# Mixture-of-experts stage of a two-block network: a split scatter, and another order of work where one expert ends and the next begins

## The reference, cut to what matters

```python
def _moe(x, w_router, w1, w3, w2):              # x: 256 x 1024
    logits = xt @ w_router                      # 8 experts, top 2 of each token
    gates = softmax(top_v)
    # for each expert: its tokens, in order
    h = silu(xg @ w1[e]) * (xg @ w3[e])         # 1024 -> 3584
    y[tokens] += (h @ w2[e]) * gate             # 3584 -> 1024
```

## Time and profile before

| what | value |
|---|---|
| median of 3 runs | 2785.34 us (2784.81 to 2785.59) |
| the profiled execution's own time | 2790.09 us |
| its span, first to last instruction | 2787.9 us |
| PE busy | 2699.8 us (97%) |
| DVE busy | 2113.8 us (76%) |
| ACT busy | 1631.4 us (59%) |
| mean granted TensorE clock | 0.996 |

### The profile page before, as it was taken

One profiled execution on the slowest core, in us unless ns is written; L12 is line 12 of the kernel. 1 busy time (PEld: TensorE's weight loads), 2 busy tenths in 40 slices (PEclk: granted clock), 3 DMA queues, 4 the chain that ended last, 5 costly groups with the idle time before them and its releaser, 6 DMA issues.

```text
span 2787.9 us, 44756 instructions
## 1 busy us (share of the span) xinstructions
PE 2699.8 (97%) x19124; PEld 2300.6 (83%) x19124; DVE 2113.8 (76%) x2117; ACT 1631.4 (59%) x1639; POOL 144.9 (5%) x152
## 2 busy tenths in 40 slices
PE   8999999999999999999999999999889999998999
PEld 7977898897788787887878787878678988877997
DVE  6677655657788888898989898877666866866685
ACT  4555443455467677676767676746545654654563
POOL 1000000000000000000000000000420000051000
PEclk9999999999999999999999999999999999999999
DMA  6345454544479898988988999953114445312443
GB/s 220 136 155 182 178 185 168 180 151 157 144 266 349 343 346 342 349 343 328 357 333 340 341 355 348 361 198 123 67 59 173 183 175 179 122 63 85 168 181 106
DMA packets 90510, 616.16 MB, mean 221 GB/s; under 512 B 10704, under 2 KB 10960, under 8 KB 20656
## 3 DMA queue, kind: packets, MB, share of 16 engines
q1 hardware_dynamic: 85392, 598.61, 58.0%
q0 software_dynamic: 4896, 14.36, 2.2%
HBM read 611.88 MB, written 1.05 MB: 220 GB/s over the span
## 4 chain that ended last, share of the span: by engine, by line
PE 82%; DVE 11%; ACT 4%; issue 2%; DMA 0%; SPq 0%; DVEq 0%; ACTq 0%
PE ps L701 24%; PE ps L703 23%; PE ps L702 23%; DVE wlo L1741 3%; ACT whi L1323 1%; PE ps L1006 1%; PE ps L1037 1%; PE ps L1183 1%; PE ps L1027 1%; ACT s L1626 1%; PE ps L1162 1%; PE ps L1194 1%; DVE s L2110 0%; DVE cin L2447 0%; ACT Q L1706 0%
## 5 line engine op out<-in xcount | busy, mean ns | idle before, releaser
L1741 DVE TENSOR_TENSOR wlo<-raw,whi 128x2048 fp32r<-128x2048 f32 (+3 forms) x588 | 1305.7, 2226 | 413.8 <-ACT whi L1323 405.4
L1323 ACT ACTIVATE whi<-raw 128x2048 fp32r<-128x2048 f32 (+3 forms) x588 | 1092.6, 1860 | 401.0 <-PE ps L703 385.2
L701 PE MATMUL ps<-whi,xTh 128*128 128x512 f32 (+5 forms) x1464 | 573.0, 391 | 12.7 <-issue 5.1
L703 PE MATMUL ps<-whi,xTl 128*128 128x512 f32 (+5 forms) x1464 | 563.2, 385 | 0.0
L702 PE MATMUL ps<-wlo,xTh 128*128 128x512 f32 (+5 forms) x1464 | 563.1, 385 | 0.0
L701 PE MATMUL ps<-xTh,whi 128*128 128x256 f32 x1480 | 418.1, 282 | 0.0
L703 PE MATMUL ps<-xTh,wlo 128*128 128x256 f32 x1480 | 417.4, 282 | 0.0
L702 PE MATMUL ps<-xTl,whi 128*128 128x256 f32 x1480 | 417.3, 282 | 0.0
L701 PEld LDWEIGHTS ps<-whi,xTh 128*128 128x128 f32 x1464 | 278.0, 190 | 73.3 <-issue 11.2
L703 PEld LDWEIGHTS ps<-whi,xTl 128*128 128x128 f32 x1464 | 277.6, 190 | 57.8
L702 PEld LDWEIGHTS ps<-wlo,xTh 128*128 128x128 f32 x1464 | 278.2, 190 | 53.3
(11 more groups left out here) (561 smaller groups left out, 3477.7 us busy)
## 6 DMA issues: line engine op xcount, KB each, us to landing
raw<-in_units_dram SPq DMA_DIRECT2D x544, 1024.0 KB, 5.0
raw<-in_units_dram SPq DMA_DIRECT2D x18, 512.0 KB, 3.6
raw<-in_units_dram SPq DMA_DIRECT2D x6, 768.0 KB, 7.1
raw<-in_units_dram SPq DMA_DIRECT2D x8, 544.0 KB, 3.6
raw<-in_units_dram SPq DMA_DIRECT2D x6, 688.0 KB, 4.0
g<-in_b_gate_dram POOLq DMA_DIRECT2D x16, 256.0 KB, 8.4
raw<-in_units_dram SPq DMA_DIRECT2D x4, 576.0 KB, 4.5
mk<-in_c_dn_dram POOLq DMA_DIRECT2D x2, 576.0 KB, 9.7
```

The costliest lines, as they stand in the source:

```text
L701: self.e.matmul(out, ah, bh, start=start, stop=False)
L703: return self.e.matmul(out, al, bh, start=False, stop=stop)
L1323: self.e.activation(self.m.hi[u % NHL][:, 0:n], self.m.raw[u % NRAW][:, 0:n], ACT.Copy) \
L1741: self.e.tensor_tensor(self.m.lo[u % NHL][:, 0:n], self.m.raw[u % NRAW][:, 0:n], self.m.hi[u % NHL][:, 0:n].bitcast(F32), ALU.subtract) \
```

## The change

1. The scatter is split like the weight products. `sel` (0/1, exact) is turned instead of `selg`, into `selT` (two buffers, fp32r). The result of `e2` is written as a high part (ACT, `expert_high`) and a low part (DVE, `expert_low`) into the first 8 blocks of `hTe`, and a scatter is four fp32r matmuls of 512 columns. The gate is multiplied in by DVE, which does the addition to `y` as two `scalar_tensor_tensor` of 128x512. `select` makes one selection (two instructions) instead of two (four). For the first column block of `e2` the two parts are written in a new step, `rest`, after the second unit of the second block.
2. The gather of the next expert leaves its place ahead of `e2` and goes to the end of the expert, in halves of 16 matmuls (first four blocks of 128 rows, then the last four). The new order at the end of expert ex is: last unit, first half of the gather, scatter 0, opening of the next expert, scatter 1, second half of the gather, branch. The opening waits for the first half of the gather alone; the second unit waits for the rest. ACT copies both parts of the second half, DVE the low part of the first.
3. `turn` stands between the first and the second unit of an expert.
4. Splits: the second unit's split of the next expert (call the units b0, b1, b2 ...) is held back from the last `e2` unit to the opening, and that of b2 is moved ahead, to just before DVE's and ACT's part of scatter 1.
5. Counts: PE reads 3, 3 and 2 counts at three steps around the last router products; DVE reads its eight at the start of `route`.

```diff
+    def expert_sum(self, cb):
+        return [h[:, 4 * cb:4 * cb + 4, :].rearrange("p (t a) n -> p t (a n)", t=2) for h in self.hTe]
...
+            if step[0] == "u" and step[1][0] == "e2" and step[1][1] < 7 and step[1][2] == 1 and step[2] == 6:
+                hold = 1
+            elif step[0] == "open" and step[1]:
+                hold = 0
+            elif step[0] == "scatter" and step[2] == 1 and step[1] < 7:
+                hold = -1
+            elif step[0] == "begin":
+                hold = 0
+            self.end.append(len(self.units) + (step[0] == "soon") - late - hold - AHEAD * (step[0] == "embed"))
...
-            o += [("counts",)] + pr[2][1:2] + [("gather", 0)]
+            o += [("counts",)] + pr[2][1:2] + [("counted",)]
+            o += [("gather", 0, 0), ("open", 0), ("gather", 0, 4)]
...
-            o += [("begin", ex), ("turn", ex)]
+            o += [("begin", ex)]
...
+                o += e1 if cb else e1[0:1] + [("turn", ex)] + e1[1:2]
...
-            if ex < 7:
-                o += [("gather", ex + 1), ("across", ex, 6)]
-            n = 3 if ex == 7 else 7
-            if ex == 7:
-                o += e2[0][0:1] + [("across", 7, 6)]
-            o += e2[0][ex == 7:] + e2[1][0:n] + [("scatter", ex, 0)] + e2[1][n:] + [("scatter", ex, 1), ("finish", ex)]
+            o += e2[0][0:1] + [("across", ex, 6)] + e2[0][1:] + e2[1][0:2] + [("rest", ex, 0)] + e2[1][2:4]
+            if ex < 7:
+                o += e2[1][4:] + [("gather", ex + 1, 0), ("scatter", ex, 0), ("open", ex + 1), ("scatter", ex, 1)]
+                o += [("gather", ex + 1, 4)]
+            else:
+                o += [("scatter", ex, 0)] + e2[1][4:] + [("scatter", ex, 1)]
+            o += [("finish", ex)]
... (PE)
+    def counts(self, first, last):
+        if first == 0:
+            self.e.wait_ge(*self.at("cnt"))
+            self.count = []
+        for ex in range(first, last):
+            self.count.append(self.e.value_load(self.m.cnt[0:1, ex:ex + 1], min_val=0, max_val=256))
...
     def scatter(self, ex, cb):
-        ps = self.fill(("sc", ex, cb), ("y", ex, cb))
-        e.wait_ge(*self.at("selgT", ex))
+        ps, T = self.fill(("sc", ex, cb), ("y", ex, cb)), m.selT[ex % 2]
+        high, low = m.expert_sum(cb)
+        e.wait_ge(*self.at("selT", ex))
+        e.wait_ge(*self.at("hiT", "ev", "e2", ex, cb))
+        for q in range(2):
+            for s in range(self.tiles):
+                e.matmul(ps[:, q * 512:q * 512 + 512], T[:, s, q * 128:q * 128 + 128], high[:, s, :], start=(s == 0), stop=False)
         e.wait_ge(*self.at("ev", "e2", ex, cb))
         for q in range(2):
             for s in range(self.tiles):
-                ins = e.matmul(ps[:, q * 512:q * 512 + 512], m.selgT[:, s, q * 128:q * 128 + 128], m.hb[:, cb, s, :],
-                               start=(s == 0), stop=(s == self.tiles - 1))
+                ins = e.matmul(ps[:, q * 512:q * 512 + 512], T[:, s, q * 128:q * 128 + 128], low[:, s, :], start=False,
+                               stop=(s == self.tiles - 1))
... (ACT)
+            ex, d0 = a
+            for half in ((1, 0) if d0 else (0,)):
...
+    def expert_high(self, ex, cb):
+        g, n = ("e2", ex, cb), self.tiles
+        self.e.wait_ge(*self.at("full", *g))
+        self.e.activation(self.m.expert_sum(cb)[0][:, 0:n, :], bands(self.psum(*g))[:, 0:n, :], ACT.Copy) \
+            .then_inc(*self.up("a_moe", ("hiT", "ev") + g))
... (DVE)
+            ex, d0 = a
+            if d0 == 0:
+                key = ("xg", ex, 1, 0)
+                e.wait_ge(*self.at("full", *key))
+                e.tensor_copy(m.xT[1][:, 0:4, :], bands(self.psum(*key), 4)).then_inc(*self.up("d_moe", key))
...
-            e.tensor_tensor(yy, yy, bands(self.psum("sc", *a)), ALU.add).then_inc(*self.up("d_moe", ("y",) + a))
+            for t in range(2):
+                ins = e.scalar_tensor_tensor(yy[:, t, :], bands(self.psum("sc", *a))[:, t, :], m.gate[:, t, a[0]:a[0] + 1],
+                                             yy[:, t, :], ALU.mult, ALU.add)
+            ins.then_inc(*self.up("d_moe", ("y",) + a))
...
+    def expert_low(self, ex, cb):
+        g, n, (high, low) = ("e2", ex, cb), self.tiles, self.m.expert_sum(cb)
+        self.e.wait_ge(*self.at("hiT", "ev", *g))
+        self.e.tensor_tensor(low[:, 0:n, :], bands(self.psum(*g))[:, 0:n, :], high[:, 0:n, :].bitcast(F32), ALU.subtract) \
+            .then_inc(*self.up("d_moe", ("ev",) + g))
...
         for t in range(2):
-            e.tensor_scalar(m.selg[:, t, :], m.iota[:, :], m.pos[:, t, ex:ex + 1], m.gate[:, t, ex:ex + 1], ALU.is_equal,
-                            ALU.mult)
```

More of the change, by code:

```diff
@@ L175, in moe @@
             self.xs, self.iota = hl("xs", [128, 2, 1024], c0), t("iota", [128, 256], I16, c0)
[L176 to L177 removed]
+            self.sel = t("sel", [128, 2, 256], F32R, c0)
+            self.selT = [t(f"selT{k}", [128, 2, 256], F32R, c0) for k in range(2)]
             with ExitStack() as c1:
@@ L663, in do @@
             self.count_tokens()
+        elif what == "route":
+            self.counts(0, 3)
         elif what == "counts":
-            self.counts()
+            self.counts(3, 6)
+        elif what == "counted":
+            self.counts(6, 8)
         elif what == "gather":
             self.gather(*a)
+        elif what == "turn":
+            self.turn(*a)
+        elif what == "open":
+            self.open_expert(("e1", a[0], 0))
         elif what == "across":
@@ L736, in unit @@
         (xh, xl), kt, last = G.x, G.kt, j == len(G.units) - 1
-        begun = j == 0 and g == self.opened
+        begun = j == 0 and g[0] == "e1" and g[2] == 0
         if j == 0 and not begun:
@@ L752, in unit @@
             for need in G.needs:
+                self.e.wait_ge(*self.at(*need))
+        if j == 1 and g[0] == "e1" and g[2] == 0:
+            for need in G.needs[1::2]:
                 self.e.wait_ge(*self.at(*need))
@@ L976, in open_expert @@
         self.open.add(self.p.slot[g])
-        for need in G.needs:
+        for need in G.needs[0::2]:
             self.e.wait_ge(*self.at(*need))
@@ L995, in count_tokens, with gather @@
         ins.then_inc(*self.up("mm_route", ("full", "pos")))
[L997 removed]
+    def gather(self, ex, d0):
         e, m = self.e, self.m
         e.wait_ge(*self.at("sel", ex))
[L1000 to L1009 removed]
+        for half in (1, 0):
+            key = ("xg", ex, half, d0)
+            ps = self.fill(key, key)
+            for d in range(4):
+                for q in range(2):
+                    ins = e.matmul(ps[:, d * 256:d * 256 + 256], m.xs[half][:, q, (d0 + d) * 128:(d0 + d + 1) * 128],
+                                   m.sel[:, q, :], start=(q == 0), stop=(q == 1))
+            ins.then_inc(*self.up("mm_moe", ("full",) + key))
     def turn(self, ex):
         e, m = self.e, self.m
[L1013 removed]
+        e.wait_ge(*self.at("sel", ex))
+        ps = self.fill(("turn", ex), ("selT", ex))
         for s in range(2):
@@ L1433, in do @@
                 .then_inc(*self.up("a_moe", ("hiT", "hTe", ex, cb)))
+        elif what == "rest":
+            e.wait_ge(*self.at("unit", self.p.unit[("e2", a[0], 1), 0]))
+            self.expert_high(*a)
         elif what == "rms":
@@ L2360, in count_tokens, with counts @@
         e.tensor_copy(m.pos[:, :, :], ps[:, 0:16].rearrange("p (t n) -> p t n", t=2)).then_inc(*self.up("d_route", ("cnt",)))
-    def counts(self):
-        self.e.wait_ge(*self.at("cnt"))
-        self.count = [self.e.value_load(self.m.cnt[0:1, ex:ex + 1], min_val=0, max_val=256) for ex in range(8)]
+    def counts(self, first, last):
+        if first == 0:
+            self.e.wait_ge(*self.at("cnt"))
+            self.count = []
+        for ex in range(first, last):
+            self.count.append(self.e.value_load(self.m.cnt[0:1, ex:ex + 1], min_val=0, max_val=256))
     def rows_low(self):
```

68 lines of the change are left out of this document (26 added, 42 removed).

## The result

| | before | after |
|---|---|---|
| median of 16 runs each, us | 2789.41 (2784.81 to 2793.67) | 2794.07 (2789.59 to 2799.16) |
| ratio to before, 95% | | 1.0022 [1.0015, 1.0028] |
| profiled execution, us (span) | 2790.09 (2787.9) | 2793.16 (2791.0) |

The kernel is slower by 0.22%, 6 us by the ratio and 4.7 by the medians; forecast was +3.8. The median of before that the forecast started from (2785.34, three runs) was at the low end of what 16 runs show, so the absolute 2789.1 lies 5 us under the 2794.07, and the difference is what can be compared. (The absolute lies in the range of 2779 to 2796, but just outside the 2785 to 2793 that the forecast gave its own mechanism.)

A forecast was written before the change was run, and what follows sets the result against it. PE was taken to set the time, with DVE having the least room. Terms +6.2 - 1.6 - 0.8 + 0.6 - 0.6 = +3.8 us gave 2789.1 us; the eight-in-ten range was 2779 to 2796.

The forecast's parts named there:

- The wait for `y`: Ahead of `turn`: PE waits 1.93 us for a PSUM buffer until DVE has added scatter 1 to `y`.
- a sign of being wrong: The gap ahead of `turn`, forecast near 1.9 us, being missing or under 1 us would show the forecast wrong.
- The wait ahead of the opening: At an expert's end, PE waits 0.47 us for ACT's copy of the gather's first half.
- The branch: Behind the gather's second half: up to 1.4 us of idle may appear, absorbed by the 1.93 wait, so no cost.
- seven ends: Ends of experts before the next: each costs 0.9 us more, 1.5 saved against 0.47 + 1.93 waited; sum +6.2 us.
- if the branch shows beside it: Sign of a wrong forecast: a gap from the branch showing beside the wait ahead of `turn`.
- `rest` and `select` at nothing: Elsewhere in the experts: one added DVE instruction of 0.61 to 0.68 us and two fewer of 0.32 change nothing.
- Opening of expert 0: Start of expert 0: smaller count loads and an earlier gather gain 1.0 to 2.2 us, taken as 1.6.
- End of expert 7: Last scatter, ahead of DVE's statistics chain: DVE's low part comes ahead of that chain, +0.6 us.
- TensorE's clock: Rival, slower: clock halves in the wait ahead of `turn`, 1.5 us lost at each of seven, 2799.6 us; chance 0.12.
- The wait for `y` isn't there: Rival, faster: no wait for scatter 1's addition, -5.2 us in seven ends, 2777.7 to 2780.5 us; chance 0.22.
- All copies hidden: Rival, faster still: the scatter's full 1.5 us kept in seven ends, 2772.3 us; chance 0.06.

The follow-up runs named there:

- y_first: Changed kernel with b2's split held until the gather's second half, so DVE adds scatter 1 to `y` first; ratio to before 1.0009, median 2790.25 us.
- after_nb: Changed kernel without the branches (variant for more than 128 tokens left out); ratio to before 1.0018, median 2794.12 us.
- counts_back: Changed kernel with PE's and DVE's count loads back where they were before; ratio to before 1.0035, median 2799.47 us.
- open_last: Changed kernel with the opening put last, behind both scatters and both gather halves, b1 split at the second half; ratio to before 0.9970, median 2780.60 us.
- gather_back: Changed kernel with the gather back at its earlier place, `turn` and the opening last in the body; ratio to before 1.0085, median 2813.36 us.
- gather_back_quiet: `gather_back` with one added wait: SyncE loads unit b5 only once PE is through b0; ratio to before 0.9990, median 2785.82 us.
- before_in: Kernel before with `turn` and the opening moved inside the branch's body, so the two jumps are adjacent; ratio to before 1.0020.

## Why the prediction was right

**The wait for `y`: right in cause and size.** The walk put the addition of scatter 1 at 9.4 to 10.7 after time 0 and b1 at 11.33. Measured are 9.39 to 10.79 (926.38 and 927.78 less 916.99) and b1 at 11.32. The order on DVE was the cause (`y_first` takes the wait away), and the gap of the branch lies under it (`after_nb`: 1.85 alone against 1.93 forecast). In the profile after, though, the gap ahead of `turn` is only 0.47 to 0.65, under the 1 us that the forecast had named as a sign of being wrong, because PE reaches `turn` about 1 us late. The moment that sets b1 was right; the picture of one gap of 1.9 was not.

**The wait ahead of the opening: 0.38 instead of 0.47.** The opening starts at 3.24 (920.23) and the scatter's work ends 2.86 after time 0; the profile calls 0.23 of that idle, since it models the end of the matmuls.

**The branch: right to be counted at nothing in the seven ends.** Up to 1.4 was the bound; 0.9 to 1.1 showed. What was behind it, a packet of code, the forecast did not have. The sentence that named it as evidence of a wrong forecast, "if the branch shows beside it", was too strict: it shows beside the wait and costs nothing, since the two together (1.6, with the ends of the matmuls modelled before each) stand in for the wait alone, which shows as 1.85 in `after_nb`.

**Scatter 0.92 against 0.94, b3's split hidden, `rest` and `select` at nothing.** PE has no wait for DVE's or ACT's splits in a plain expert; the one wait of 0.6 for a split between 740 and 1860 stands in before as well.

**Opening of expert 0: -2.4 instead of -1.6.** The mechanism held and the size was off: the b2 product started at 801.47 against a forecast of 801.6 to 802.9, because the branch's block on ACT, taken at up to 1.33, cost nothing: ACT goes from its copies to the split without idling (797.09). The walk of PE was met within 0.2 at the gather and the opening (788.30 and 791.87 against 788.5 and 791.9). b1 was not: it starts at 798.39 against 797.4, since the gap of 1.09 behind the branch stood ahead of it and the walk had none there. It did not matter: b2's own split is ready 0.3 us after b1 is through (798.39 + 2.81 = 801.20) and sets b2's start.

**End of expert 7: +0.2 instead of +0.6.** Two short waits, of which the first was there before (0.78), and the rest of the stage moves unchanged. After:

```profile
1831.17 0.69 PE L1059 MATMUL ps<-hTeh,selT 128*128 128x512 f32 x2 [0.84 <-ACT hTeh L1762]
1832.52 0.73 PE L1063 MATMUL ps<-hTel,selT 128*128 128x512 f32 x2 [0.66 <-DVE hTel L2357]
...
1844.76 0.47 PE L823 MATMUL ps<-whi,xTh 128*128 128x512 f32 x1 [0.34 <-ACT xTh L1355]
```

DVE's low part ends well ahead of what PE needs next, and only the 0.66 of it that PE waits for, less the shorter scatter, is paid.

**Not foreseen: the long gap at expert 2, +4.6.** The prediction had no step for it. It made up for the terms above that came out better, and for the 3.1 us given back later, so part of the agreement in the sum (+3.8 forecast, +3.1 between the profiles, +4.7 between the medians) is luck. It is a second wait for code: a second packet ends at 1059.13, 1.54 us before PE goes on, and each of the eight such gaps in the study (2.15 to 3.96 us) has one, 1.26 to 1.62 before its end. It appears within a few matmuls behind a branch, it is at the same place in kernels whose code lies alike (expert 2 in after, `y_first`, `counts_back` and `open_last`), it moves when the code is shifted, and it is gone without branches. That the jump lands near the end of a block of code at that place fits all of this; the trace doesn't hold the addresses, and no run took this gap away alone. The forecast's seven ends add up to 6.3 from its own 0.90, not 6.2; nothing hangs on it.

**The rivals.** TensorE's clock did not fall in the waits of this forecast: even the unbroken 1.85 of `after_nb` was followed by matmuls 0.23 apart, and in the experts of after it fell only behind the 3.75 (granted 0.55). "From about 2 us on it decides" was too simple: it fell behind 2.37 in `open_last` and stayed at 1.00 behind 2.96 in `gather_back`. "The wait for `y` isn't there" was false for this kernel, and `y_first` shows its price: 128.8 to 129.1 from expert to expert. The forecast had put that case at 0.7 under before's 128.79, with nothing behind the branch; the 0.88 to 1.14 that show there take it back. Its clause "because DVE's part comes earlier" was the right place to look: it is one line in the list. "All copies hidden" was false for the order as changed; `open_last` is nearly that case, and was reached by an order I hadn't considered.

## What to carry to other kernels

When a step of PE is moved, walk the helper engines in their own order for the one instruction that frees a PSUM buffer PE is about to take: here 1.4 us of adding stood behind 2.3 us of splitting, which cost 0.8 us at each of seven ends (129.66 against 128.9 in `y_first`). Put the longest run of independent matmuls last ahead of a branch and short ones first, and look at the DMA share at the jump: the same branch cost 0.5 to 0.8 us with quiet queues and 2.6 to 4.6 with loads in flight. Where a gap has no releaser in the profile ("issue"), look for a DMA packet of kind "instruction" that ends shortly before it does. Before an edit is judged by its total, compare it at several points of the span, since one gap at one place (4.6 us) was as large as the change.

## What the runs showed of the hardware

A jump of PE over the body of an expert has no fixed price. Behind it PE was idle for 0.17 to 0.81 us (`open_last`), 0.50 to 0.80 (`gather_back_quiet`), 0.9 to 1.1 (after), 2.6 to 4.6 (`gather_back`), with 3 us of matmuls or more queued ahead each time. What PE waits for is a packet of code of 16.4 KB: it takes 0.9 to 1.6 us as a rule (up to 2.6 beside a second one), and PE goes on 1.26 to 1.68 us after its end in 84 of 87 gaps. The Trainium skill (Advanced Engine Details and Errata, Control Flow Timing) has about 108 ns for a compare-and-branch. No run here prices that instruction by itself; by the packets the gaps of 0.17 to 4.6 are those of the code.

Gaps of 2.15 to 4.0 us, "issue", stand a few matmuls behind a branch at one or two places of a kernel, each with a second packet of code, and the place goes with the order of the code and not with the work.

TensorE's granted clock fell from 1.00 to 0.55 (2.4 to 1.2 GHz for most of the stretch) behind an idle of 3.75 us that followed one of 0.90, and not behind a wait of 1.85 us. In between, the length of one idle doesn't tell: the clock fell behind 2.37 (`open_last`) and 2.44 (before), and not behind 2.41 (`before_in`) or 2.96 (`gather_back`).
